# GpSimd's scatter of a pass ahead of its gather, the accumulating scatter ahead of the plain one, and the first tile's sums added after the last pass

## The reference

```python
scores = jax.nn.sigmoid((t @ w_router).astype(jnp.float32))
...
_, top_e = lax.top_k(jnp.where(expert_mask, biased, -jnp.inf), TOP_K)      # 8 of 64 experts
wts = wts / jnp.sum(wts, axis=-1, keepdims=True) * ROUTED_SCALE
...
def expert_block(args):
    tok, wb, e = args
    xb = t_pad[tok]
    yb = swiglu(xb, w_e_gate[e], w_e_up[e], w_e_down[e])
    return yb * wb[:, None]
...
routed = jax.ops.segment_sum(yb.reshape(P, d), slot_tok, num_segments=T + 1)[:T]
shared = swiglu(t, w_sh_gate, w_sh_up, w_sh_down)
return (routed + shared).astype(h.dtype).reshape(b, n, d)
```

## Time and profile before

| | us |
|---|---|
| median of 3 runs | 1007.27 |
| lowest, highest | 1006.61, 1007.97 |
| the profiled execution, its time | 1007.2 |
| the profiled execution, its span | 1005.4 |
| PE busy (93%) | 938.9 |
| DVE busy (52%) | 520.6 |
| POOL busy (46%) | 462.3 |
| ACT busy (33%) | 330.3 |

### The profile page before, as it was taken

The page is one execution under the profiler, slowest core; times in us unless marked ns, Lnnn a source line. Parts: engine busy times, 40 slices in busy tenths (PEclk is TensorE's granted clock), DMA queues, the critical chain, the costliest instruction groups (busy, mean ns, idle before and its releaser), DMA issues. The chain is left out here.

```text
span 1005.4 us, 14543 instructions
## 1 busy us (share of the span) xinstructions
PE 938.9 (93%) x4307; PEld 405.4 (40%) x4308; DVE 520.6 (52%) x717; ACT 330.3 (33%) x591; POOL 462.3 (46%) x342
## 2 busy tenths in 40 slices
PE   3999999999999999999999989998999999989875
PEld 1644444677456543333333333332333333333322
DVE  1336779786267954444443444444444333444457
ACT  4212222576345412232232222332222233222322
POOL 0312432000000147666776775765776676766611
PEclk9999999999999999999999989998999999999978
DMA  9955442420325969999979999999999999999775
GB/s 371 355 206 209 168 178 94 187 119 1 139 83 199 388 241 354 397 398 389 395 287 404 408 398 388 402 395 378 407 361 358 382 366 379 365 368 349 214 290 154
DMA packets 68448, 299.69 MB, mean 298 GB/s; under 512 B 21518, under 2 KB 22514, under 8 KB 39361
## 3 DMA queue, kind: packets, MB, share of 16 engines
q1 hardware_dynamic: 41522, 261.16, 65.5%
q0 software_dynamic: 25840, 35.98, 13.6%
q10 hardware_dynamic: 1056, 2.18, 0.6%
HBM read 284.78 MB, written 62.91 MB: 346 GB/s over the span
## 5 line engine op out<-in xcount | busy, mean ns | idle before, releaser
L1274 PE MATMUL psum<-wring,xres 128*64 (+1 forms) x1664 | 373.8, 602 | 17.5 <-DVE wring L1754 16.1
L581 POOL DMA_INDIRECT xg<-h_rows,gidx x208 | 256.5, 1233 | 179.5 <-issue 92.7
L1758 DVE STREAM_TRANSPOSE xres<-xg 128x1024 f32<-128x1024 f32 x52 | 106.4, 2046 | 259.4 <-DMA xg<-h_rows,gidx 258.5
L1274 PEld LDWEIGHTS psum<-wring,xres 128*64 128x64 f32 x1664 | 120.7, 139 | 234.7 <-issue 234.6
L1286 PE MATMUL psum<-wring,rows 128*64 x416 | 189.7, 599 | 7.8 <-DVE rows L1792 6.9
L1286 PE MATMUL psum<-rows 128*64 128x512 f32 x416 | 189.7, 599 | 0.0
L893 ACT COPY xres<-psum 128x1024 f32<-128x1024 f32 x52 | 52.6, 1012 | 278.4 <-DMA expert_sums<-xres,sidx 238.9
L1754 DVE COPY wring<-wring 128x1536 f32 x104 | 123.0, 1224 | 16.1 <-SPq L465 14.6
L1286 PEld LDWEIGHTS psum<-wring,rows 128*64 128x64 f32 x416 | 57.4, 138 | 126.5 <-issue 126.5
L832 ACT COPY rows<-wring 128x1024 f32 x104 | 103.5, 1046 | 7.9 <-PE psum L1286 7.5
L591 POOL DMA_INDIRECT expert_sums<-xres,sidx x50 | 81.8, 1636 | 15.2 <-issue 15.2
(11 more groups left out here) (273 smaller groups left out, 919.8 us busy)
## 6 DMA issues: line engine op xcount, KB each, us to landing
wring<-in_w_e_gate SPq DMA_DIRECT2D x64, 1024.0 KB, 8.5
wring<-in_w_e_up SPq DMA_DIRECT2D x64, 1024.0 KB, 15.1
wring<-in_w_e_down SPq DMA_DIRECT2D x64, 1024.0 KB, 17.3
ring<-in_w_ada SPq DMA_DIRECT2D x20, 1024.0 KB, 5.2
wring<-expert_sums SPq DMA_DIRECT2D x8, 1024.0 KB, 11.7
ring<-in_w_in SPq DMA_DIRECT2D x3, 2048.0 KB, 25.7
heads<-in_w_ada SPq DMA_DIRECT2D x4, 1024.0 KB, 23.3
ring<-in_w_out SPq DMA_DIRECT2D x1, 4096.0 KB, 12.7
```

The costliest lines, as they stand in the source:

```text
L581: pool.indirect_dma_start(xg[q][:, 256 * s:256 * s + 256], None, hrows, bass.IndirectOffsetOnAxis(gidx[:, q, s:s + 1].bitcast(U32), 0), bo ...
L1274: last = pe.matmul(pp[2][SUB * g:SUB * g + SUB, 512 * q:512 * q + 2 * F] .rearrange("p (u f) -> p u f", u=2), xT[:, q, k, SUB * g:SUB * g ...
L1758: dve.transpose(xT[:, q].rearrange("p k (s r) -> p s k r", s=4), xg[q].rearrange("p (s r k) -> p s k r", s=4, k=KD)).then_inc(s_xte, 1)
```

## The change

Three edits. In `scatter` the accumulating DMA is issued before the plain one. In the two starting passes and in the loop `scatter` is called before `gather`, so that GpSimd issues the scatter of pair p-2 and then the gather of pair p+2. At the end DVE runs `add_sums(0)` after the last `keep_hidden` instead of before it.

```diff
@@ -585,12 +585,12 @@
             def scatter(p, q, rows_of_pair, indices_set):
                 pool.wait_ge(s_si, indices_set)
                 pool.sem_inc(s_pgo, 1)
+                pool.indirect_dma_start(sums, bass.IndirectOffsetOnAxis(sidx[:, q, 1:2].bitcast(U32), 0),
+                                        rows_of_pair, None, bounds_check=PARTS * T - 1, oob_is_err=False,
+                                        compute_op=ALU.add).then_inc(s_scat[q], 16)
                 pool.indirect_dma_start(sums, bass.IndirectOffsetOnAxis(sidx[:, q, 0:1].bitcast(U32), 0),
                                         rows_of_pair, None, bounds_check=PARTS * T - 1, oob_is_err=False)\
                     .then_inc(s_scat[q], 16)
-                pool.indirect_dma_start(sums, bass.IndirectOffsetOnAxis(sidx[:, q, 1:2].bitcast(U32), 0),
-                                        rows_of_pair, None, bounds_check=PARTS * T - 1, oob_is_err=False,
-                                        compute_op=ALU.add).then_inc(s_scat[q], 16)
@@ -609,8 +609,8 @@
             for p in range(2):
+                scatter(p - 2, p, arow[:, 3], p + 1)
                 gather(p + 2, p, p + 2)
-                scatter(p - 2, p, arow[:, 3], p + 1)
@@ -619,8 +619,8 @@
                 for q in range(2):
+                    scatter(i + (q - 2), q, ysb[:, q], i + (q + 1))
                     gather(i + (q + 2), q, i + (q + 2))
-                    scatter(i + (q - 2), q, ysb[:, q], i + (q + 1))
@@ -1838,8 +1838,6 @@
-                if k == -1:
-                    add_sums(0)
@@ -1865,6 +1863,7 @@
+            add_sums(0)
             add_sums(1)
```

## The result

The changed kernel is slower, by less than one per cent. Over 19 runs each its median is 1013.81 us (1010.4 to 1016.88) against 1008.14 us (1006.02 to 1012.46) of before; the ratio of the two kernels is 1.0041 with a 95% interval of 1.0027 to 1.0055. That is 2.7 to 5.5 us more by the ratio, and 5.7 us by the medians. I had forecast 11 us less.

The account below looks back on a forecast made before the run. A two-pass loop of gather, scatter and keep_y waits was taken to bound the last 21 passes. Gains of 9 (loop, capped by weights), 1.2 (last scatter) and 1.0 us (sums) gave 11.2: from 1007.2 to 996.0 us, range 990 to 1007.

Parts of the forecast that it names:

- The size of a gather's landing: Loop passes: transpose follows the gather's first issue by 11.39 to 11.94 us, at most 1.35 us later close behind a scatter.
- T - Z: Transpose of the next pair (T) minus the pass's silu (Z); forecast -0.7 us, upper bound +0.6.
- the 13.3: Passes 28 to 49: us lost because 21 passes took 238.8 us instead of 10.74 each; TensorE alone could win about 11.
- K: Start of ACT's keep_y in a pass; forecast 3.51 us after the silu in every pass, no longer waiting for scatters.
- DVE's weight copy: Runs 2.37 us; the fourth gather issue meets it and loses 0.9 us, or all 2.37 by the Trainium skill.
- Rival B: GpSimd's queue: gather moves only once the scatter ahead has landed, landing 16 us after first issue; 1019 us, chance 0.12.
- Before pass 28 it costs next to nothing: Scatter-gather loop in early passes: the second block's weights were late, so time won earlier would be waited out there.
- The weights' cap of 9 us: Pass 51: last up weights land at 943.3 us regardless of TensorE, so the loop's gain is capped at about 9 us.
- a loop of 22.73 us: Two passes: gather start, scatter issue 9.65, landing and keep_y 9.12, next gather 3.96; 11.37 us per pass against TensorE's 10.74.
- the stall rule T - Z - 0.13: A pass grows by transpose time minus silu time minus 0.13 us when positive, by nothing when the transpose is earlier.
- C: Rival: the weight stream keeps up, so all 13.3 us come back and some of pass 50's stall; 991.5 us, chance 0.10.
- A: Rival: a pass's software DMAs take the queue about 11.4 us however ordered, only the tail gains; 1005.0 us, chance 0.18 (with losses up to the forecast).

Follow-up runs that it names:

- acc_first: The kernel before, with the accumulating scatter issued ahead of the plain one and the gather still ahead of both; 1011.76 us, ratio 1.0044.
- order_only: The kernel before, with scatter called ahead of gather and the plain half still ahead of the accumulating one; 1014.60 us, ratio 1.0077.
- after_delay: The changed kernel with four short memsets on GpSimd (some 2 us) between scatter and gather of each loop pass; 1045.03 us in one run.
- order_2_to_13: The kernel before, with scatter ahead of gather in passes 2 to 13 only, plain half first; 1009.22 us, ratio 1.0011.
- tail_only: The kernel before, with add_sums(0) moved behind the last keep_hidden and nothing else; 1007.57 us, ratio 1.0005.
- early_index: The kernel before, with ACT setting the gather's indices for pair p+3 right after the silu of pass p; 1000.20 us, ratio 0.9918.
- early_index_tail: The kernel before, with gather indices set right after the silu and add_sums(0) moved behind the last keep_hidden; 999.58 us, ratio 0.9932.
- after_early_index: The changed kernel, with ACT setting the gather's indices right after the silu; 1015.87 us, ratio 1.0066.
- after_no_add: The changed kernel, with the accumulating scatter made a plain one that writes its rows instead of adding; 991.04 us in one run.

## Why the prediction was wrong

*The size of a gather's landing: the step that failed.* I took 11.39 and 11.94 us after the gather's first issue as a latency and moved it with the issue, with 1.35 us more as the upper bound. Close behind a scatter it is mostly the time until the queue has worked off what stands ahead, and counted from the end of the scatter ahead it hardly changes: 14.6 (before), 15.0 (acc_first), 15.5 (order_only), 15.3 (after) and 14.3 us (after_delay), in kernels whose gathers start 0.3 to 3.0 us behind, while from the gather's own issue it goes from 11.3 to 15.2. The two rows that I compared hid this: their gathers stood 7.07 and 2.61 us behind the scatter ahead, and none stood close. I also took the wrong gap for my upper bound. The 1.65 us belong to the gather of 808.39; the one that landed in 11.94 (797.09) has 2.61. With 2.31 us instead of 1.35 for the lost gap, T - Z is +1.6, a pass grows by 0.5 us, and 10 us of the 13.3 are gone.

The rest of that step's formula held. The changed kernel has its first gather at K + 5.7 (forecast 5.3) and its transpose 15.0 us later. Then T - Z without stalls is 3.51 + 5.7 + 15.0 - 21.47 = 2.7, and a pass grows by (2.7 - 0.13)/3 = 0.86 us. Late passes took 11.59, that is 0.85 more than 10.74. With 14.6 from the scatter's end (2.61 + 11.94 in the earlier trace rows) the same sum is 3.51 + 5.0 + 14.6 - 21.47 = 1.6 and 0.5 us per pass: some 3 us left to gain in the loop where I had taken 9.

The 0.9 us that I feared from DVE's weight copy, and 2.37 us at worst, didn't come: the gather's four issues take 5.0 us in the late passes of the changed kernel, less than the 6.3 of before. It is now the scatter that sometimes meets the copy (1.77 us at 801.37).

*Rival B named the mechanism and was mispriced.* It had the gather wait for the whole landing of the scatter ahead, at 16 us and 1019 us, and 0.12 of the chance. The landing came to 15.0, just where I had put the point of decision ("about 15 us"), and the loop came out even with before in the late passes. I gave B little because of 0.5 us between two rows. Of the gather's last issue I should have asked the same: from its end to the transpose the time went from 6.1 to 10.0 us, the 4 us that I had denied. B's sum has an error as well. Its 552 us run to the silu of pass 50 (952.05) and contain TensorE's wait for weights ahead of it, which its 566 us leave out; from silu 1 to silu 49 the passes take 547, so that B's price was 19 us on equal terms, before the 2.2 of the end. The rule of the Trainium skill that I cited against the change (DMA: Bandwidth & Descriptors, Queues, rings and completion order), that a ring's descriptors are consumed in order, agrees with after_delay, where a gather issued 2.7 us later landed no later behind its scatter.

*"Before pass 28 it costs next to nothing": failed as well.* I looked at TensorE's waits for weights, which swallow time that TensorE wins or loses, but not at the load that waits for TensorE. SP can't issue the loads of expert 22 until the products of pass 13 are done, because expert 16 holds their place in the ring. The 3.7 us lost from pass 1 to 13 were not swallowed at pass 28 (0.7 more lost there). That this is the order's doing is what the profiles say: pass 1 to 13 took 135.7, 135.1 and 135.5 us in the changed kernel, order_only and order_2_to_13, against 132.0 in the kernel before and 133.7 in tail_only. In the time of order_2_to_13 it could not be told from nothing.

*The weights' cap of 9 us* was never reached by the change. early_index, which cuts both loops, gained 8, and the two kernels without accumulation 17 and 22 in a single run each. So a cap worked out from the weights' arrival held only for the mix of other DMAs that it was read in.

*Right:* K at Z + 3.51 and the end of ACT's waits; the scatter at K + 2.25 (forecast 2.0); the bound of the last 21 passes by a loop of 22.73 us, which early_index confirms by cutting it; the stall rule T - Z - 0.13; and, in the profile, the end. From the silu of pass 49 on it gains 2.9 us against 2.2: 1.7 for the last scatter (1.2 forecast), 1.4 from its landing to the last instruction (1.0 forecast for the sums), less 0.1 ahead of it. No time shows the sums' part: tail_only and early_index_tail can't be told from the kernels without it. *C* fell with the forecast, and *A* fell to early_index, where the same DMAs in another rhythm took 10.74 and 11.00 us per pass.

## What to carry to other kernels

When an issue is moved within one software queue, count a DMA's landing from the end of the DMA ahead of it as well as from its own issue, in several passes with different gaps, down to the gap that the change will make. Here the first hardly moved for gaps up to 3 us and the second decided at 7 us, and neither held in early_index, where more than a pass of DMAs was queued. A wait is removed cheaply by making its input ready earlier: here the gather's buffer was free at 800.00 (797.96 + 2.04 in the earlier trace rows), 8.4 us before its next gather began, and setting the indices earlier won 8 us with GpSimd's order untouched. And where a stall seems to swallow a loss, look for transfers that are released by the slowed engine ahead of it.

## What the runs showed of the hardware

- A gather of 128 rows in four indirect DMAs, next to weight loads (the DMA engines' share was 1.01 from 800 to 900 us, in after_delay 0.92), was there 14.3 to 15.5 us after the end of the scatter ahead, whether its first issue came 0.3 or 3.0 us behind (late passes of before, after, acc_first, order_only, after_early_index and after_delay). After a gap of 7.07 us it was there 11.4 us after its own first issue, 18.5 after the scatter's end. Where the DMA engines had less to do (share 0.53, after_delay, 840 to 860 us) one was there 8.1 us after its own issue.
- In this kernel accumulation went with longer landings: a gather behind a scatter 15.3 us after the scatter's end with it and 13.9 without (after, after_no_add), at a busy share of the DMA engines of 1.01 and 0.99. The issue of an accumulating scatter took 1.60 us against 1.02 of a plain one.
- The queue worked off four gathers and two scatters per 11.0 us with accumulation (passes 37 to 49 of early_index).
